# Products of the identity in TensorE's waits behind three layer norms of a two-layer decoder step

## The reference

```python
for l in range(DEPTH):                       # DEPTH = 2
    mix = attention_mix if l % 2 == 0 else gla_mix
    xp = layer_norm(DN_ALPHA * xp + mix(xp), ln_mix_g[l], ln_mix_b[l])      # and xs
    f = conv_ffn(xp, ...)   # up to value|gate (2 x 2816), causal conv of 3, silu gate, down
    xp = layer_norm(DN_ALPHA * xp + f, ln_ffn_g[l], ln_ffn_b[l])            # and xs
```

## Time and profile before

| what | us |
|---|---|
| three timed runs | 1568.86, 1576.65, 1576.21 |
| their median | 1576.21 |
| the profiled execution's own time | 1568.5 |
| its span, first to last instruction | 1566.6 |
| TensorE busy | 1474.9 |
| mean granted TensorE clock | 0.981 |

### The profile page before, as it was taken

The page is one execution under the profiler, slowest core; times in us unless marked ns, Lnnn a source line. Parts: engine busy times, 40 slices in busy tenths (PEclk is TensorE's granted clock), DMA queues, the critical chain, the costliest instruction groups (busy, mean ns, idle before and its releaser), DMA issues.

```text
span 1566.6 us, 24257 instructions
## 1 busy us (share of the span) xinstructions
PE 1474.9 (94%) x9372; PEld 1307.8 (83%) x9372; DVE 910.2 (58%) x1734; ACT 562.6 (36%) x1062; POOL 60.9 (4%) x91
## 2 busy tenths in 40 slices
PE   6999898799999999999989999979899999999995
PEld 5888666579999999887788888758899999998784
DVE  2654264286666666536541777765766666664546
ACT  2222177424333333323323443541343333333231
POOL 0002100010000000000000100110100000000000
PEclk9999999898999999999999999999999999999998
DMA  5334456552222222312212211272122222214211
GB/s 178 104 101 132 108 213 234 179 112 81 81 80 80 80 80 80 118 67 95 79 56 81 81 54 54 85 235 56 55 81 80 80 80 80 80 54 131 82 67 61
DMA packets 153215, 153.56 MB, mean 98 GB/s; under 512 B 12014, under 2 KB 122734, under 8 KB 152910
## 3 DMA queue, kind: packets, MB, share of 16 engines
q1 hardware_dynamic: 149210, 139.47, 29.0%
q0 software_dynamic: 3936, 13.14, 2.5%
HBM read 140.76 MB, written 21.91 MB: 104 GB/s over the span
## 4 chain that ended last, share of the span: by engine, by line
PE 84%; DVE 6%; ACT 3%; issue 2%; SPq 2%; DMA 2%; POOL 1%; ACTq 0%; DVEq 0%; POOLq 0%
PE ps L701 69%; PE ps L712 5%; PE ps L682 3%; PE ps L1061 1%; PE ps L769 1%; PE ps L803 1%; ACT w_hi L1201 1%; SPq L553 1%; DVE x_reg L1782 1%; DVE x_reg L1786 1%; DVE xl_reg L1580 1%; DVE w_lo L1573 1%; PE ps L982 1%; POOL w_lo L2174 1%; DVE x_reg L1764 1%
## 5 line engine op out<-in xcount | busy, mean ns | idle before, releaser
L701 PE MATMUL ps<-xh_reg,w_hi 128*128 128x288 f32 x1552 | 463.6, 299 | 8.6 <-DVE xl_reg L1580 5.1
L701 PE MATMUL ps<-xh_reg,w_lo 128*128 128x288 f32 x1552 | 459.4, 296 | 0.0
L701 PE MATMUL ps<-xl_reg,w_hi 128*128 128x288 f32 x1552 | 459.3, 296 | 0.0
L701 PE MATMUL ps<-w_hi,xh_reg 128*128 128x512 f32 x768 | 307.2, 400 | 6.9 <-DVE xl_reg L1823 3.4
L701 PEld LDWEIGHTS ps<-xh_reg,w_hi 128*128 128x128 f32 x1552 | 293.6, 189 | 11.0 <-issue 6.2
L701 PE MATMUL ps<-w_hi,xl_reg 128*128 128x512 f32 x768 | 301.3, 392 | 0.0
L701 PE MATMUL ps<-w_lo,xh_reg 128*128 128x512 f32 x768 | 301.2, 392 | 0.0
L701 PEld LDWEIGHTS ps<-xl_reg,w_hi 128*128 128x128 f32 x1552 | 293.7, 189 | 0.0
L701 PEld LDWEIGHTS ps<-xh_reg,w_lo 128*128 128x128 f32 x1552 | 293.4, 189 | 0.0
L1573 DVE TENSOR_TENSOR w_lo<-raw,w_hi 128x2048 fp32r<-128x2048 f32 (+1 forms) x51 | 111.4, 2184 | 257.0 <-ACT w_hi L1201 257.0
L1201 ACT ACTIVATE w_hi<-raw 128x2048 fp32r<-128x2048 f32 (+1 forms) x55 | 100.9, 1834 | 223.0 <-PE ps L712 214.6
(11 more groups left out here) (205 smaller groups left out, 1462.7 us busy)
## 6 DMA issues: line engine op xcount, KB each, us to landing
raw<-in_ffn_w_up SPq DMA_DIRECT2D x88, 512.0 KB, 5.0
raw<-in_ffn_w_down SPq DMA_DIRECT2D x40, 512.0 KB, 4.5
raw<-in_attn_w_in SPq DMA_DIRECT2D x24, 512.0 KB, 4.8
raw<-in_gla_w_in SPq DMA_DIRECT2D x24, 512.0 KB, 4.5
out_swa_s<-in_state_swa_kv SPq DMA_DIRECT2D x2, 3968.0 KB
x_reg<-in_x_prompt SPq DMA_DIRECT2D x8, 512.0 KB, 7.1
raw<-in_gla_w_out SPq DMA_DIRECT2D x8, 512.0 KB, 4.6
arena<-in_state_gla SPq DMA_DIRECT2D x3, 1024.0 KB, 5.8
```

The lines of the kernel that those rows point to most:

```text
L701: mm = pe.matmul(out, lhs(i, a), rhs(i, b), start=first and i == 0 and a + b == 0, stop=last and i == ks - 1 and a == 1)
```

## The change

It adds a function `fill(n)` to PE's program, which issues n products of the 128x128 identity with itself, in float32, into the first 128 columns of bank 7, and calls it at three places of `run_here`: 8 at m = 0 ahead of the wait for the low halves; 12 at m = 2, behind the side turns (where there are any) and ahead of the wait for the last tile's norm; 10 behind that tile's turn and ahead of the waits for its copies. `run_here` runs behind three norms, so 90 products are added. Nobody reads their result and they signal no semaphore.

```diff
+            def fill(n):
+
+                for _ in range(n):
+                    pe.matmul(ps[:, 7, 0:P], ident[:, :], ident[:, :], start=True, stop=True)
+
             def run_here(m, stage, first_batch):
 
 
                 if m == 0:
+                    fill(8)
                     lo_here(first_batch, 6)
                 elif m == 1:
                     after_ln(stage, [3])
                 elif m == 2:
                     if stage % 2 == 0:
                         turn_sides(stage // 2)
+                    fill(12)
                     after_ln(stage, [4])
+                    fill(10)
                     pe.wait_ge(turned_out, first_batch + TURNS_X + (0 if stage % 2 else 2))
                     lo_here(first_batch, TURNS_X)
```

## The result

The changed kernel is slower. Six runs have a median of 1582.06 us (1580.37 to 1582.51) against 1574.43 (1568.86 to 1576.65, six runs) before; the ratio is 1.005, 95% interval 1.0033 to 1.0067. I had forecast about +3 us, a time of 1576 (range 1568 to 1583), and gave "slower by over 0.5%" 0.09. A later group of ten runs of the changed kernel gave 1580.06 against 1575.26, ratio 1.0031 (1.0012 to 1.0051). Both say slower, by 5 to 8 us.

A forecast was written before the change was run, and what follows sets the result against it. TensorE (PE), busy 94% of the span, was taken to bound the kernel. Norm terms -1.3+3.0+0.7 gave +2.4 us (+6.5 with the clock lost), taken as +3: 1571.5 or 1579.2 by level, forecast 1576, range 1568 to 1583.

The forecast's parts named there:

- A: Norm behind attn_out, near 340 us: fills cost 1.2 us, give back 2.5 if the clock is kept, net -1.3.
- C: Norm behind gla_out, near 1110 us: fills cost +2.3 us, net +0.7 if the clock is kept.
- I take nearly all of the saving and little of the loss.: Choice of +3 us between sums of +2.4 and +6.5, as the clock's fall can shift by microseconds.
- rival 2: Clock falls in the side transposes all the same, so fills only cost: +6.5 us, 1575.1 (1582.8); chance 0.15.
- The price: One identity product on PE: 0.21 us at full clock, 0.43 at half; 8, 12 and 10 take 1.7, 2.5, 2.1.
- The first fill: The 8 products ahead of each norm's first run: +0.6 us in A, +1.7 in B and in C.
- B: Norm behind down0, near 787 us: fills cost +3.0 us and nothing is given back.
- Rival 3: Fills run at half clock and do not bring it back: +17.3 us, 1585.8 (1593.5); chance 0.07.
- Rival 1: Fills lie in the waits and the clock never falls: -5.6 us, 1562.9 (1570.6 by the upper pair); chance 0.07.
- The page: Skill text: transposes don't count as busy to the clock like products; by it the sum would be rival 2's.
- The level of times: Four known times of the kernel before: two at 1568.5 to 1568.9 us, two at 1576.2 to 1576.7.

The follow-up runs named there:

- the second trace: The changed kernel, unaltered, profiled once more against the kernel before: 1580.06 us against 1575.26, ratio 1.0031.
- run 2: Not a follow-up kernel: the third run of products on PE in the stage behind a norm, after tile 4's turn; before, 2.14 us behind that turn in A.
- run 0: Not a follow-up kernel: the first run of products on PE in the stage behind a norm, after POOL's split and the fill of 8.
- the fitted fills: Kernel before plus fills sized to each wait, the first moved ahead of the weights' wait: 1568.18 us against 1575.26, ratio 0.9958; again 1568.21 against 1575.59.
- the first group: Kernel before, unchanged, on the same chip as some of the follow-up kernels: 31 runs, median 1574.32 us.

## Why the prediction was wrong

- **The size.** I forecast +3 us with bounds of +2.4 (clock kept in A and C) and +6.5 (not kept). The norms cost 7.65 and 4.45 us in two traces, the first of them more than the upper bound, and the times say +7.6 and +4.8. The measured 1582.06 is inside the range, but the forecast of 1576 was no change against the 1576.21 I compared with, and the kernel is slower; the value between the bounds was drawn too near the better one. Besides, the middle of 1571.5 and 1579.2 is 1575.35, not 1576.
- **The step that failed: "I take nearly all of the saving and little of the loss."** In both traces of the changed kernel C lost the clock, 0.5 and 0.4 us into the fill of 12, and in one A lost it too, inside the sides. In A that is rival 2's mechanism, to which I gave 0.15; in C I had reasoned that the fill covers the wait in which the clock fell before, and it fell all the same. The fill of 12 then took 4.3 to 4.6 us where I had 2.5. In return the clock was back before the fill ended and the products behind it ran at full clock, 0.13 us apart, which rival 2 had not counted. Norm C net: +0.7 forecast, +2.95 measured twice. Of the 2.25 us between them, 2.0 lie ahead of tile 4's turn (3.9 us late, 1.9 forecast) and 0.35 in the fill of 10; the products gave back 1.7, as forecast (1.6).
- **The price.** 8, 12 and 10 products push what follows by 1.8, 2.8 to 2.9 and 2.3 us at full clock (341.82-340.01 in A; 795.47-792.69 in B of the kernel with its 8 moved and 353.76-350.88 in A of the second trace; 359.36-357.11), 0.23 each where I took 0.21. At half clock the 0.43 that I took was right. And the turn of tile 4 holds PE for 357.11-356.47 = 0.64 us, not 0.4. From turn to run 2 it is 2.9 us where I had 2.5. Together these are 0.018 x 90 = 1.6 us and three times 0.24, 0.7 us: 2.3 us at most, if all of it pushes what follows. Norm A of the second trace, where the clock was kept, shows what this does alone: -0.6 measured, -1.3 forecast.
- **The first fill** was placed rightly: forecast +0.6, +1.7 and +1.7, measured +0.64, +1.83 and +1.81 in the second trace. That it stands behind the wait it should fill is most of the loss: alone it makes the kernel slower by 0.26%, and moved ahead of the wait the changed kernel is no slower than before. I had this term in the sum; what I set against it was the saving.
- **Norm B:** +3.0 forecast, +3.7 and +2.1 measured; "the half-clock stretch that now stretches products will stretch fills" is what the first trace shows. The second had none, which I had given as possible. So the +2.1 holds a gain against before: tile 4's turn stands there at 14.86 us behind the start of POOL's split, and at 13.3 in six other traces that had kept the clock until then. It is no sign that the terms of B were too large.
- **Rival 3** is wrong: the clock came back under the fill of 12 at 355.2 us in A and 1136.8 in C, so products of the identity do not keep it down. In B it came back at 792.1, 0.9 us behind the start of run 0, so that rise says nothing of the fills. **Rival 1** is wrong for this kernel, though the fitted fills come near to it in B.
- **The page.** In norm A the clock fell inside the small transposes with PE never idle. The Trainium skill, "TensorE: Matmul & The Clock Gate", Part 4, has transposes count for the clock otherwise than products; these rows agree, and by that rule rival 2 deserved more than 0.15. For the full-width transposes, which the earlier trace rows left open, the measurement differs from the page. In the trace with the fill of 12 alone:

```profile
284.86 3.44 PE L682 MATMUL ps<-ident,x_reg 128*128 128x128 f32 x16 [6.69 <-DMA x_reg<-in_state_swa_kv]
...
287.00:289.00 2.00, 2.00 (x26) 1.56 (x25) 0.00 (x0) 1.55 (x3) 0.00 (x0) 0.81 1.06 408
```

PE had idled for 6.69 us and then ran nothing but these transposes until 288.24, and the clock rose at 287.8 (0.50 until then, by the 0.81 of the window). So such transposes can raise it, and the small ones did not hold it.
- **The level of times.** I spoke of two levels, 1568.7 and 1576.4, from four runs. The 31 runs of before in the first group go from 1568.73 to 1580.11 with no gap over 2.1 us; there are no two levels. The spread goes with the clock: the four with a mean granted clock of 0.974 or 0.975 took 1577.35 to 1580.11 us, the eight with 0.980 or 0.981 took 1568.73 to 1574.32.

## What to carry to other kernels

A filler only helps if it stands ahead of the wait that it is to fill: look at which semaphore ends the idle time in the timeline, and put the filler ahead of that wait in the engine's queue. Size it by the measured spacing of the like instruction at full clock, so that it ends before the idle time does. What overflows is paid in full (8 behind the wait of B: 1.83 us), and nearly twice where the clock is down (10 products: 2.25 and 4.3 us). Before filling a wait, ask what the wait is for: here a root stood behind a copy in another engine's queue, and moving it gave 4.1 us by the medians where all fitted fills gave 7.1.

## What the runs showed of the hardware

The granted clock can fall with PE busy throughout, under small transposes: PE is busy for all of 350 to 352 us in the changed kernel, and the clock falls at 351.8. It came back under dense products of the identity (at 355.2 us), and in another trace under full-width transposes (at 287.8 us). Products that have just begun behind the small transposes did not prevent the fall either: it came at 1133.4 us, 0.5 us into a fill. And the same program keeps or loses the clock from one execution to the next at nearly the same place: at 1036 to 1038 us the mean is 1.00 in one trace of before and 0.55 in another. Runs of that program spread over 11 us, and most of it goes with the granted clock. So one pair of profiled executions, 13.5 us apart here, says little of a change worth 5. Cut out the stretches that the change touches and compare those.
